# The layers' normalised input from the joined split parts of the turned x, in place of a second turn on TensorE

## The chip, the cores and the metric

One Trainium2 chip, one core (program of one core). The metric is device time in microseconds (us), the median of several executions. Engines: TensorE (PE, weight loads apart as PEld), VectorE (DVE), ScalarE (ACT), GpSimd (POOL) and the DMA queue of SyncE (SP).

## The reference, cut to what matters

A float32 network on 256 tokens of 2048 channels: a macaron block (feed-forward, token mixing, feed-forward), then two layers of a second block, each conditioned by an adaptive norm. The change touches only the opening of these two layers:

```python
for l in range(2):
    shift, scale, gate = split(silu(c) @ w_ada[l] + b_ada[l])          # per channel
    h = x * rsqrt(mean(x * x, axis=-1) + eps) * norm_g[l]              # per token rstd
    h = h * (1 + scale) + shift
    pieces = h @ w_in[l]                                               # 2048 x 6656, 13 pieces of 512
    ...                                                                # four mixers
    x = x + gate * (concat(mixers) @ w_out[l])
```

All products are done to float32 accuracy: both operands are split into a rounded high part and a low part, and three of the four partial products are summed.

## The kernel before, in words

The weights stream through as 1045 slabs of 512 KB. SP loads slab n into one of four stage buffers as soon as the low part of slab n - 4 is made. ScalarE rounds it into the high part (L1604), and GpSimd (L870, `rest`) or VectorE (L2111, `slab_lo`) subtracts to make the low part. TensorE runs the hi passes of a slab (16 products), waits for the low part, and runs the lo passes (8 products). Every engine works through an order of its own that is written out in the program; semaphores couple them.

A layer begins at slab `S_LAY[l]` (here called slab 0). Its h = x^T * gain * rstd + shift must lie with channels on partitions, and the sum over all channels that `rstd` needs is ready only when the last feed-forward or output group has been added to x. So the first two groups of products (8 slabs, `raw_product` with q = 0 and 1) run on the raw, unscaled turned x: `round_raw` (ScalarE) and `rest_raw` (VectorE, L2053) have made `hi + lo = x^T * gain`, block by block of 512 channels (`raw_views`). Blocks 0 to 2 are turned early; block 3 is turned by TensorE (`turn_raw`) behind slab 0. The results of the two groups are scaled by `rstd` afterwards (`raw_evacuate`).

The other groups take the real h. To make it, the kernel before computes `rstd` on VectorE from the sum of squares (`mean`, L1975, then `rstd_of`, L1981 to L1986: half, reciprocal, square, step, result; each two elements per partition), scales x by it per token (`scale_x`, L2071, 8 instructions of 128x512 a layer), turns the scaled x on TensorE once more (`turn_scaled`, transposes recorded at L908, 8 behind each slab of group 1), adds gain and shift on ScalarE (`gain_h`, L1664), and splits it on VectorE (`split_h`: casts L2063, subtract L2065). Group 2 waits for `h_ready` of each block.

`rstd` along the tokens of every partition (`rstd_b`) is made by two small diagonal matrices (`rdiag`, L2099), one product with ones behind group 0 (L1012) and a copy out of PSUM (L2517). The first two `turn_scaled` wait for that copy, since the banks of PSUM are shared.

In a layer VectorE makes the low parts of all input slabs but 0, 1, 6, 8 and 10, which are GpSimd's (`RAW_BY_POOL`). So between slab 1 and slab 6 GpSimd has nothing to do. On SP's queue the loads of the slabs and small rows of a bias table alternate; the other half of the rows is issued by GpSimd behind slab 10.

Of the kernel before, what the change touches and what calls it, by code (L numbers as in the profile page):

```python
# [283 lines left out]
def build(nc, a, out, const, marks, final):  # L284

    ctx = ExitStack()
    with ctx:
# [9 lines left out]
        def signal(name):  # L297
            return Signal(sem(name), marks.setdefault(name, {}), final)
# [77 lines left out]
        lgt, w2 = u(LGT, P, 3, 32), u(W2C, P, 2, 2, DH)  # L376
        y = u(CY, P, TT, D)
        yrs = u(YRS, P, S)
# [32 lines left out]
        def shifted(b):  # L411
            return u(LSQ + 1024 * (b % 2), P, 4, S)
# [19 lines left out]
        ada_split_done, ada_picked = sem("ada_split_done"), sem("ada_picked")  # L432
        block_turned = signal("block_turned")
        token_half, x_half, gained, h_rounded = (signal(n) for n in ("token_half", "x_half", "h_gained", "h_rounded"))
        h_ready, turned, squared, mean_done, root_done, rstd_ready, scaled, rounded = (signal(n) for n in (
# [430 lines left out]
        def _(pool):  # L866
            def rest(n):
# [3 lines left out]
                                        slab_part(n, 0, size(n)).bitcast(F32), ALU.subtract).then_inc(lo_pool, 1)  # L871

            for n in range(S_END):
                if n == S_MIX + 8:
                    pool.wait_ge(slab_done, S_MIX)
                    pool.wait_ge(ada_red, ADA_GROUPS)
                    pool.dma_start(U[:, DIST:DIST + MIX_END - BASE_END], const[:, BASE_END:MIX_END]).then_inc(mix_in, 16)
                    for kv in range(2):
                        pool.dma_start(w2[:, kv], a["cmp_w2"][0, kv].rearrange("(c p) n -> p c n", p=P)).then_inc(mix_in, 16)
# [7 lines left out]
                for l in range(2):  # L887
                    if n == S_LAY[l] + MASKED:
                        pool.wait_ge(*turned.after(3 + l, 3))
                        if l == 1:  # L890
# [12 lines left out]
        def _(pe):  # L903
# [77 lines left out]
            def raw_product(l, q):  # L981
# [5 lines left out]
                for k in range(4):  # L987
# [15 lines left out]
                    if q == 0 and k == 0:  # L1003
# [3 lines left out]
                        turn_raw(l, 3, 1).then_inc(*turned.mark("raw", l, 3))  # L1007
                    if q == 1:
                        turn_scaled(r, k)
                if q == 0:  # L1010
                    pe.wait_ge(*vec_out.after("rdiag", l))
                    mm(ps[:, 5, 0:S], ones, u(LNX, P, S), start=True, stop=True).then_inc(*pe_out.mark("scales", l))  # L1012

# [120 lines left out]
            def turn(r, b, src, T):  # L1134
# [3 lines left out]
                return last  # L1138

            def turn_scaled(r, b):  # L1140

                if b > 1:
                    pe.wait_ge(*gained.after(r, b - 2, 1))
                else:
                    pe.wait_ge(*vec_out.after("rstd_b", r - 3))
                for T in range(TT):
                    pe.wait_ge(*scaled.after(r, b, T))
                    last = turn(r, b, y, T)
                last.then_inc(*turned.mark(r, b))

# [432 lines left out]
        def _(act):  # L1583
# [72 lines left out]

            def gain_h(r, b, gain, shift):

                act.wait_ge(*turned.after(r, b))
                if b > 1:  # L1660
                    act.wait_ge(*h_ready.after(r, b - 2))
                for c in range(4):
                    m = 4 * b + c
                    last = fn(shifted(b)[:, c, :], turn_bank(r, b, c // 2)[:, c % 2, :], ACT.Identity, scale=gain[:, m:m + 1],  # L1664
                              bias=shift[:, m:m + 1])
                    if c % 2:
                        last.then_inc(*gained.mark(r, b, c // 2))
# [196 lines left out]
            for l in range(2):  # L1864
# [8 lines left out]
                for b in range(4):  # L1873
                    round_upto(s0 + 7 + b)
                    gain_h(3 + l, b, ascale[:, l, :], mod[:, l, 0:16])
                for p in range(PIECE + 1):
# [88 lines left out]
        def _(dve):  # L1965
# [101 lines left out]

            def scale_x(r, b):
                for T in range(TT):
                    cols = slice(b * WN, (b + 1) * WN)  # L2070
                    v.tensor_scalar(y[:, T, cols], x[:, T, cols], rstd[:, r, T:T + 1], None, ALU.mult).then_inc(*scaled.mark(r, b, T))  # L2071

# [16 lines left out]
            def norm_layer(l):  # L2089

                r, s0 = 3 + l, S_LAY[l]
                mean(r)
                rstd_of(r)
                dve.wait_ge(*rstd_ready.after(r))
                slab_lo(s0 + 2)
                rest_raw(l, 3)
                slab_lo(s0 + 3)
                for T in range(TT):
                    last = v.tensor_scalar(u(LNX, P, TT, P)[:, T, :], ident, rstd[:, r, T:T + 1], None, ALU.mult)  # L2099
                last.then_inc(*vec_out.mark("rdiag", l))  # L2100
                scale_x(r, 0)
                slab_lo(s0 + 4)
                for b in range(1, 4):
                    scale_x(r, b)
                slab_lo(s0 + 5)
# [398 lines left out]
            for l in range(2):  # L2504
# [6 lines left out]
                def raw_evacuate(q):  # L2511
# [3 lines left out]
                    if q == 0:  # L2515
                        dve.wait_ge(*pe_out.after("scales", l))
                        chained(v.tensor_copy(rstd_b[:, :], ps[:, 5, 0:S]), "rstd_b", l)  # L2517
                        dve.wait_ge(*vec_out.after("pad", l))
# [314 lines left out]
```

## Time and profile before

| | us |
|---|---|
| median of 3 runs | 3048.07 (3046.91 to 3048.76) |
| span of the profiled execution, first to last instruction | 3042.5 |
| median less span | 5.6 |
| TensorE busy in the span | 3022.6 (99%) |
| VectorE busy | 2007.6 (66%) |
| ScalarE busy | 1450.9 (48%) |
| GpSimd busy | 1305.0 (43%) |
| openings of layers 0 and 1 in the span | about 2171 to 2202 and 2600 to 2632 |

Times of the trace count from the start of the span. The span is one execution; the median is of others, so a forecast is made as a difference against the span and carried to the median.

### The profile page before, as it was taken

How to read it: one execution, taken by the hardware profiler on the slowest of the kernel's cores; microseconds unless marked ns; L12 is line 12 of the kernel's file. 1: busy time of each engine (PE TensorE's matmuls, PEld its weight loads, DVE VectorE, ACT ScalarE, POOL GpSimd, SP SyncE). 2: the span in 40 equal slices, each digit the busy share in tenths (PEclk: the TensorE clock that was granted, in tenths of full speed). 3: DMA queues.
4: the chain of work that ended last, by engine and by line, in shares of the span. 5: the costliest groups of instructions: out<-in, count | busy, mean ns of one | idle time of the engine just before them, and what ended most of it. 6: DMA issues, size and time to landing. Idle time of an engine off the chain costs nothing.

```text
span 3042.5 us, 46560 instructions
## 1 busy us (share of the span) xinstructions
PE 3022.6 (99%) x18776; PEld 2678.1 (88%) x18776; DVE 2007.6 (66%) x2956; ACT 1450.9 (48%) x1886; POOL 1305.0 (43%) x646
## 2 busy tenths in 40 slices
PE   9999999999999999999999999999999999999998
PEld 7888888888999999998888888888899998999997
DVE  4777666664324447786567666577579866689764
ACT  6444444444667455544544444444544454534454
POOL 5454545445565555594554444444350004510013
PEclk9999999999999999999999999999999999999999
DMA  7888887886776555555788888787576546665555
GB/s 233 277 277 259 270 281 250 286 288 180 229 174 177 157 167 147 155 171 194 231 269 275 271 268 269 259 287 267 172 213 193 156 144 214 175 191 181 153 179 181
DMA packets 495535, 663.28 MB, mean 218 GB/s; under 512 B 74312, under 2 KB 281912, under 8 KB 494808
## 3 DMA queue, kind: packets, MB, share of 16 engines
q1 hardware_dynamic: 485704, 655.83, 68.2%
q0 software_dynamic: 4448, 2.94, 0.3%
q8 instruction: 148, 2.42, 0.3%
q10 hardware_dynamic: 5168, 1.53, 0.2%
q14 instruction: 67, 0.55, 0.1%
HBM read 655.99 MB, written 2.11 MB: 216 GB/s over the span
## 4 chain that ended last, share of the span: by engine, by line
PE 97%; DMA 1%; DVE 1%; ACT 0%; POOL 0%; issue 0%; DVEq 0%; ACTq 0%
PE ps L1056 36%; PE ps L918 20%; PE ps L1061 18%; PE ps L924 10%; PE ps L935 3%; PE ps L940 1%; PE ps L908 1%; PE ps L1548 1%; DMA stage<-in_w_in 1%; PE ps L1332 1%; PE ps L1313 1%; PE ps L995 0%; PE ps L1027 0%; PE ps L1158 0%; POOL narrow_split_slabs L870 0%; PE ps L1370 0%
## 5 line engine op out<-in xcount | busy, mean ns | idle before, releaser
L870 POOL TENSOR_TENSOR split_slabs<-stage,split_slabs 128x1024 fp32r<-128x1024 f32 x318 | 777.6, 2446 | 1300.8 <-ACT split_slabs L1604 1300.6
L1604 ACT ACTIVATE split_slabs<-stage 128x1024 fp32r<-128x1024 f32 x592 | 627.4, 1061 | 870.4 <-PE ps L1061 813.5
L1056 PE MATMUL ps<-split_slabs,h_split 128*128 128x512 f32 x3288 | 813.6, 389 | 0.0
L1604 ACT ACTIVATE narrow_split_slabs<-stage 128x1024 fp32r<-128x1024 f32 (+1 forms) x437 | 457.3, 1051 | 620.4 <-PE ps L924 459.4
L1056 PEld LDWEIGHTS ps<-split_slabs,h_split 128*128 128x128 f32 x3288 | 616.8, 188 | 128.3
L2111 DVE TENSOR_TENSOR split_slabs<-stage,split_slabs 128x1024 fp32r<-128x1024 f32 x274 | 356.6, 1302 | 463.7 <-ACT split_slabs L1604 462.0
L918 PE MATMUL ps<-h_split,narrow_split_slabs 128*128 128x256 f32 x4928 | 623.6, 279 | 0.0
L918 PEld LDWEIGHTS ps<-h_split,narrow_split_slabs 128*128 128x128 f32 x4928 | 589.0, 188 | 11.5 <-issue 6.6
L870 POOL TENSOR_TENSOR narrow_split_slabs<-stage,narrow_split_slabs 128x1024 fp32r<-128x1024 f32 (+1 forms) x184 | 445.2, 2430 | 347.7 <-ACT narrow_split_slabs L1604 347.5
L1061 PE MATMUL ps<-split_slabs,h_split 128*128 128x512 f32 x1644 | 439.5, 389 | 0.0
L2111 DVE TENSOR_TENSOR narrow_split_slabs<-stage,narrow_split_slabs 128x1024 fp32r<-128x1024 f32 x253 | 329.2, 1304 | 138.2 <-ACT narrow_split_slabs L1604 137.8
L1061 PEld LDWEIGHTS ps<-split_slabs,h_split 128*128 128x128 f32 x1644 | 308.6, 188 | 64.4
L1056 PE MATMUL ps<-split_slabs,act_split 128*128 128x512 f32 x1392 | 344.1, 389 | 0.0
L924 PE MATMUL ps<-h_split,narrow_split_slabs 128*128 128x256 f32 x2464 | 332.7, 278 | 0.0
L1056 PEld LDWEIGHTS ps<-split_slabs,act_split 128*128 128x128 f32 x1392 | 261.3, 188 | 54.5
L924 PEld LDWEIGHTS ps<-h_split,narrow_split_slabs 128*128 128x128 f32 x2464 | 305.2, 188 | 0.0
L1061 PE MATMUL ps<-split_slabs,act_split 128*128 128x512 f32 x696 | 186.1, 389 | 0.0
L2173 DVE STREAM_TRANSPOSE ps<-U 32x256 f32<-32x256 f32 x352 | 160.3, 455 | 5.0
L1061 PEld LDWEIGHTS ps<-split_slabs,act_split 128*128 128x128 f32 x696 | 130.7, 188 | 27.3
L2127 DVE SCALAR_TENSOR_TENSOR ps<-U,cact,ps 128x512 f32<-128x512 f32 x192 | 145.1, 756 | 6.8
L2124 DVE SCALAR_TENSOR_TENSOR ps<-U,cact,ps 128x512 f32<-128x512 f32 x168 | 126.1, 751 | 22.5 <-DMA U<-in_w_ada 20.2
L2549 DVE SCALAR_TENSOR_TENSOR U<-U,params 128x256 f32<-128x256 f32 x240 | 112.1, 508 | 0.0
(307 smaller groups left out, 2540.2 us busy)
## 6 DMA issues: line engine op xcount, KB each, us to landing
stage<-in_ffn_w_gu SPq DMA_DIRECT2D x352, 512.0 KB, 4.9
stage<-in_w_in SPq DMA_DIRECT2D x349, 512.0 KB, 3.8
U<-in_w_ada SPq DMA_DIRECT2D x192, 512.0 KB, 5.4
stage<-in_ffn_w_down SPq DMA_DIRECT2D x176, 512.0 KB, 5.0
stage<-in_w_out SPq DMA_DIRECT2D x96, 512.0 KB, 4.1
stage<-in_w_in SPq DMA_DIRECT2D x80, 128.0 KB, 2.9
stage<-in_w_branch_c SPq DMA_DIRECT2D x32, 192.0 KB, 3.4
stage<-in_cmp_w SPq DMA_DIRECT2D x8, 512.0 KB, 5.1
```

Of the source, the lines that this page charges most:

```text
L870: nc.gpsimd.tensor_tensor(slab_part(n, 1, size(n)), stage[:, n % RING, 0:size(n)], slab_part(n, 0, size(n)).bitcast(F32), ALU.subtract).th ...
L918: mm(bank[:, c * S:(c + 1) * S], w[0][:, kk, at:at + P], moving(kk, i), start=first and c == 0 and kk == 0 and i == 0, stop=False)
L924: ins = mm(bank[:, c * S:(c + 1) * S], w[1][:, kk, at:at + P], moving(kk, 0), start=False, stop=last and c == outs - 1 and kk == chunks - 1)
L935: mm(bank[:, T * W2:(T + 1) * W2], hx[:, i, KC * k + kk, T * P:(T + 1) * P], w[0][:, kk, :], start=k + T + kk + i == 0, stop=False)
L1056: mm(ps[:, 2 * pair + T, :], stationary(kk, i)[:, T * P:(T + 1) * P], w[0][:, kk, :], start=first and kk == 0 and i == 0, stop=False)
L1061: ins = mm(ps[:, 2 * pair + T, :], stationary(kk, 0)[:, T * P:(T + 1) * P], w[1][:, kk, :], start=False, stop=last and kk == WK - 1)
L1604: return fn(slab_part(n, 0, size(n)), stage[:, n % RING, 0:size(n)], ACT.Copy)
L2111: v.tensor_tensor(slab_part(n, 1), stage[:, n % RING, :], slab_part(n, 0).bitcast(F32), ALU.subtract).then_inc(lo_vec, 1)
L2124: ins = v.scalar_tensor_tensor(total, w[:, 0, :], cact[:, 2 * k:2 * k + 1], total, ALU.mult, ALU.add)
L2127: v.scalar_tensor_tensor(total, w[:, 1, :], cact[:, 2 * k + 1:2 * k + 2], total, ALU.mult, ALU.add).then_inc(ada_load, 1)
L2173: last = v.transpose(dst[turned_rows, :, :, rows], src[rows, :, :, turned_rows])
L2549: ins = v.scalar_tensor_tensor(cy[:, c, :], src, col, cy[:, c, :], ALU.mult, ALU.add)
```

## The change

The second turn is dropped. Since the split parts of the raw turned x already add up to x^T * gain, GpSimd adds them back into one plain tensor (`join_raw`, 128x1024 a block, into `plain_h`, which takes the place of `y`); VectorE multiplies it in place by `rstd_b` (`scale_h`); ScalarE only adds the shift (`shift_h`). The split stays. In layer 0 the last 128 channels of the high part lie in a place of their own, so block 3 is joined in two pieces. GpSimd does the joins between its low parts of slabs 1 and 6. On TensorE the product that spreads the scales moves from behind slab 3 to behind slab 1, and on VectorE `rdiag` moves ahead of the low part of slab 2, the copy of `rstd_b` out of the evacuation of group 0 to behind the low part of slab 3. ScalarE does `shift_h` one slab earlier in its order than `gain_h` was.

```diff
+            def join_raw(l, b):
+                pool.wait_ge(*h_ready.after("raw", l, b))
+                m0, m1 = 4 * b, 4 * b + 4
+                if (l, b) == (0, 3):
+                    m1 = DC - 1
+                    nc.gpsimd.tensor_tensor(plain_h[:, m1, :], raw_part(l, 0, m1)[:, 0:S].bitcast(F32), raw_part(l, 1, m1)[:, 0:S].bitcast(F32), ALU.add
+                                            ).then_inc(*joined.mark(l, "last"))
+                lo_at = raw_views[l][2]
+                parts = [raw_views[l][0][:, at + m0 * XW:at + m1 * XW].rearrange("p (c w) -> p c w", c=m1 - m0)[:, :, 0:S].bitcast(F32) for at in (0, lo_at)]
+                nc.gpsimd.tensor_tensor(plain_h[:, m0:m1, :], parts[0], parts[1], ALU.add).then_inc(*joined.mark(l, b))
+
             for n in range(S_END):
+                for l in range(2):
+                    if n == S_LAY[l] + 2:
+                        pool.wait_ge(slab_done, S_LAY[l])
+                        for b in range(4):
+                            join_raw(l, b)
...
                     if n == S_LAY[l] + MASKED:
-                        pool.wait_ge(*turned.after(3 + l, 3))
+                        pool.wait_ge(*gained.after(3 + l, 3, 1))
...
-                    if q == 1:
-                        turn_scaled(r, k)
-                if q == 0:
-                    pe.wait_ge(*vec_out.after("rdiag", l))
-                    mm(ps[:, 5, 0:S], ones, u(LNX, P, S), start=True, stop=True).then_inc(*pe_out.mark("scales", l))
+                    if q == 0 and k == 1:
+                        pe.wait_ge(*vec_out.after("rdiag", l))
+                        mm(ps[:, 5, 0:S], ones, u(LNX, P, S), start=True, stop=True).then_inc(*pe_out.mark("scales", l))
...
-            def gain_h(r, b, gain, shift):
-                act.wait_ge(*turned.after(r, b))
+            def shift_h(r, b, shift):
+                act.wait_ge(*scaled.after(r, b))
...
-                    last = fn(shifted(b)[:, c, :], turn_bank(r, b, c // 2)[:, c % 2, :], ACT.Identity, scale=gain[:, m:m + 1],
-                              bias=shift[:, m:m + 1])
+                    last = fn(shifted(b)[:, c, :], plain_h[:, m, :], ACT.Identity, bias=shift[:, m:m + 1])
...
-                    round_upto(s0 + 7 + b)
-                    gain_h(3 + l, b, ascale[:, l, :], mod[:, l, 0:16])
+                    round_upto(s0 + 6 + b)
+                    shift_h(3 + l, b, mod[:, l, 0:16])
...
+            def scale_h(l, b):
+                dve.wait_ge(*joined.after(l, b))
+                if (l, b) == (0, 3):
+                    dve.wait_ge(*joined.after(l, "last"))
+                part = plain_h[:, 4 * b:4 * b + 4, :]
+                v.tensor_tensor(part, part, by_token(4), ALU.mult).then_inc(*scaled.mark(3 + l, b))
...
                 rstd_of(r)
                 dve.wait_ge(*rstd_ready.after(r))
+                for T in range(TT):
+                    last = v.tensor_scalar(u(LNX, P, TT, P)[:, T, :], ident, rstd[:, r, T:T + 1], None, ALU.mult)
+                last.then_inc(*vec_out.mark("rdiag", l))
                 slab_lo(s0 + 2)
                 rest_raw(l, 3)
                 slab_lo(s0 + 3)
-                for T in range(TT):
-                    last = v.tensor_scalar(u(LNX, P, TT, P)[:, T, :], ident, rstd[:, r, T:T + 1], None, ALU.mult)
-                last.then_inc(*vec_out.mark("rdiag", l))
-                scale_x(r, 0)
+                dve.wait_ge(*pe_out.after("scales", l))
+                chained(v.tensor_copy(rstd_b[:, :], ps[:, 5, 0:S]), "rstd_b", l)
+                for b in range(3):
+                    scale_h(l, b)
                 slab_lo(s0 + 4)
-                for b in range(1, 4):
-                    scale_x(r, b)
+                scale_h(l, 3)
                 slab_lo(s0 + 5)
```

## Rows read from the trace of the kernel before

**Rows 1.** The page: its head and the chain that ended last

```profile
span 3042.5 us, 46560 instructions
...
PE 97%; DMA 1%; DVE 1%; ACT 0%; POOL 0%; issue 0%; DVEq 0%; ACTq 0%
```

**Rows 2.** Waits of TensorE, 2165 to 3042: total, times, longest

```profile
PE ps L908 <- DVE rstd_b L2517: 4.0, 2, 2.3
```

**Rows 3.** Timeline of weight loads, layer 0: start, us, instructions, count, [idle before]

```profile
2178.40 1.98 PEld L995 LDWEIGHTS ps<-raw_split,narrow_split_slabs 128*128 128x128 f32 x16
...
2186.49 1.03 PEld L1000 LDWEIGHTS ps<-raw_split,narrow_split_slabs 128*128 128x128 f32 x8
2189.41 0.86 PEld L908 LDWEIGHTS ps<-base_consts,U 128*128 128x128 f32 x8 [1.90 <-DVE rstd_b L2517]
2190.23 1.98 PEld L995 LDWEIGHTS ps<-raw_split,narrow_split_slabs 128*128 128x128 f32 x16
...
2193.11 0.90 PEld L908 LDWEIGHTS ps<-base_consts,U 128*128 128x128 f32 x8
...
2193.98 1.97 PEld L995 LDWEIGHTS ps<-raw_split,narrow_split_slabs 128*128 128x128 f32 x16
```

**Rows 4.** The same timeline, layer 1

```profile
2606.79 2.00 PEld L995 LDWEIGHTS ps<-raw_split,narrow_split_slabs 128*128 128x128 f32 x16
...
2614.93 1.02 PEld L1000 LDWEIGHTS ps<-raw_split,narrow_split_slabs 128*128 128x128 f32 x8
2618.50 1.57 PEld L908 LDWEIGHTS ps<-base_consts,U 128*128 128x128 f32 x8 [2.55 <-DVE rstd_b L2517]
2620.05 2.72 PEld L995 LDWEIGHTS ps<-raw_split,narrow_split_slabs 128*128 128x128 f32 x16
```

**Rows 5.** Windows: busy us of each engine (count), granted clock, DMA share, GB/s

```profile
2187.52:2190.23 2.71, 1.02 (x9) 0.82 (x8) 2.68 (x9) 1.41 (x2) 2.28 (x1) 1.00 0.47 145
...
2615.95:2620.05 4.10, 1.76 (x10) 1.55 (x9) 3.18 (x9) 2.94 (x3) 1.65 (x1) 0.78 1.08 329
```

**Rows 6.** Timeline of VectorE in the openings of both layers

```profile
2173.76 0.17 DVE L1981 TENSOR_SCALAR newton<-meansq 128x2 f32<-128x2 f32 x1
...
2174.75 0.16 DVE L1986 SCALAR_TENSOR_TENSOR rstd<-newton 128x2 f32<-128x2 f32 x1
...
2178.39 1.23 DVE L2111 TENSOR_TENSOR narrow_split_slabs<-stage,narrow_split_slabs 128x1024 fp32r<-128x1024 f32 x1
...
2179.53 0.48 DVE L2099 TENSOR_SCALAR U<-base_consts,rstd 128x128 f32<-128x128 f32 x2
...
2189.00 0.36 DVE L2517 COPY rstd_b<-ps 128x256 f32<-128x256 f32 x1
...
2604.69 0.17 DVE L1981 TENSOR_SCALAR newton<-meansq 128x2 f32<-128x2 f32 x1
...
2607.18 1.66 DVE L2053 SCALAR_TENSOR_TENSOR raw_split<-ps,ascale,raw_split 128x256 fp32r<-128x256 f32 x4
```

**Rows 7.** Timeline of GpSimd in the openings of both layers

```profile
2170.56 2.41 POOL L870 TENSOR_TENSOR narrow_split_slabs<-stage,narrow_split_slabs 128x1024 fp32r<-128x1024 f32 x1 [0.31 <-ACT narrow_split_slabs L1604]
...
2187.95 3.22 POOL L870 TENSOR_TENSOR narrow_split_slabs<-stage,narrow_split_slabs 128x1024 fp32r<-128x1024 f32 x1 [14.98 <-ACT narrow_split_slabs L1604]
...
2601.69 2.39 POOL L870 TENSOR_TENSOR narrow_split_slabs<-stage,narrow_split_slabs 128x1024 fp32r<-128x1024 f32 x1 [1.76 <-ACT narrow_split_slabs L1604]
```

**Rows 8.** Timeline at two other places of the kernel, VectorE beside GpSimd

```profile
1198.01 2.36 DVE L2393 TENSOR_TENSOR rden<-rden,gn 128x6 f32<-128x6 f32 x1
...
1468.16 3.21 POOL L870 TENSOR_TENSOR split_slabs<-stage,split_slabs 128x1024 fp32r<-128x1024 f32 x1
1469.03 2.37 DVE L1981 TENSOR_SCALAR newton<-meansq 128x2 f32<-128x2 f32 x1
```

**Rows 9.** Timeline of ScalarE: the rounding of slab 6 in layers 0 and 1

```profile
2186.81 1.06 ACT L1604 ACTIVATE narrow_split_slabs<-stage 128x1024 fp32r<-128x1024 f32 x1 [1.14 <-DMA stage<-in_w_in]
...
2618.85 1.06 ACT L1604 ACTIVATE narrow_split_slabs<-stage 128x1024 fp32r<-128x1024 f32 x1 [0.53 <-DMA stage<-in_w_in]
```

More of the change, by code:

```diff
@@ L376, in build @@
         lgt, w2 = u(LGT, P, 3, 32), u(W2C, P, 2, 2, DH)
-        y = u(CY, P, TT, D)
+        plain_h = u(CY, P, DC, S)
         yrs = u(YRS, P, S)
@@ L433, in build @@
         block_turned = signal("block_turned")
+        joined = signal("raw_parts_joined")
         token_half, x_half, gained, h_rounded = (signal(n) for n in ("token_half", "x_half", "h_gained", "h_rounded"))
@@ L1138, in turn @@
                 return last
[L1140 to L1145, printed above, removed]
-                for T in range(TT):
-                    pe.wait_ge(*scaled.after(r, b, T))
-                    last = turn(r, b, y, T)
-                last.then_inc(*turned.mark(r, b))
             def ada_reduce(f, b):
@@ L2066, in split_h @@
                                 ).then_inc(*h_ready.mark(r, b))
[L2068 to L2071, printed above, removed]
+            def scale_h(l, b):
[4 more added lines that the diff above has]
+                v.tensor_tensor(part, part, by_token(4), ALU.mult).then_inc(*scaled.mark(3 + l, b))
             def norm_mix():
@@ L2097, in norm_layer @@
                 slab_lo(s0 + 3)
-                for T in range(TT):
-                    last = v.tensor_scalar(u(LNX, P, TT, P)[:, T, :], ident, rstd[:, r, T:T + 1], None, ALU.mult)
-                last.then_inc(*vec_out.mark("rdiag", l))
-                scale_x(r, 0)
+                dve.wait_ge(*pe_out.after("scales", l))
+                chained(v.tensor_copy(rstd_b[:, :], ps[:, 5, 0:S]), "rstd_b", l)
+                for b in range(3):
+                    scale_h(l, b)
                 slab_lo(s0 + 4)
-                for b in range(1, 4):
-                    scale_x(r, b)
+                scale_h(l, 3)
                 slab_lo(s0 + 5)
@@ L2515, in raw_evacuate @@
                     if q == 0:
-                        dve.wait_ge(*pe_out.after("scales", l))
-                        chained(v.tensor_copy(rstd_b[:, :], ps[:, 5, 0:S]), "rstd_b", l)
                         dve.wait_ge(*vec_out.after("pad", l))
```

## The prediction

> **What bounds the kernel now.** The chain that ended last is 97% TensorE, and the span is 3042.5 us [rows 1]. So only time in which TensorE waits or does other work than products can move the end. The view of waits, cut to the part from the last down-projection slab on, holds one line for TensorE: it waits for `rstd_b` (L2517), once in each layer, 4.0 us in all [rows 2]. Behind the layer openings it waits for nothing, so a shift of TensorE there goes through to the end at full size. I then read the two openings in the timeline by engine.
>
> In layer 0 slab 4 (the first of raw group 1) is done at 2186.49 + 1.03 = 2187.52, the first `turn_scaled` starts at 2189.41 after 1.90 us idle, and slab 5 starts at 2190.23 [rows 3]. A raw slab takes 2193.11 - 2190.23 = 2.88 us (24 weight loads, the last 8 need the slab's low part), a turned block of 8 transposes 2193.98 - 2193.11 = 0.87 us. Layer 1 is alike, but its wait is 2.55 us, and there the first block takes 1.57 us instead of 0.87 and the next 16 weight loads 2.72 us instead of 1.98 [rows 3, 4]. The view of windows tells why: the granted clock of that stretch is 0.78 of full speed (half speed, 1.2 GHz, for part of it), and 1.00 in layer 0's [rows 5]. So this dip costs 0.70 + 0.74 = 1.4 us.
>
> **What the change removes.** 64 transposes and both waits. Layer 0: 1.90 + 0.82 + 3 x 0.87 = 5.3 us. Layer 1: 2.55 + 1.4 + 4 x 0.87 = 7.4 us. In all 12.7 us, if nothing else comes late. The scales product only moves, and 16 `scale_x` of 0.48 us on VectorE turn into 8 `scale_h` of the size of a slab's low part, 1.23 us [rows 6]: 2 us more on VectorE. ScalarE's `shift_h` reads SBUF in place of PSUM, taken as equal; it now stands one slab earlier in the queue and has its input long before. SP's order of issues is the same, but its load of slab 6 waits for slab 2's low part, of slab 7 for slab 3's, of slab 8 for slab 4's; POOL's bias rows wait for the last `shift_h` in place of the last turn, and nothing near is queued behind them.
>
> **What it adds.** GpSimd gets four joins per layer (layer 0: the last in two pieces). The nearest row is its own low-part subtract, the same two inputs in SBUF and 128x1024: 2.41 us [rows 7]; I take that, with 0.6 and 1.8 us for the pieces. Before, GpSimd was idle 14.98 us there, from 2172.97 on [rows 7]. The joins of blocks 0 to 2 wait for data ready long ago, so they run back to back behind slab 1's low part: 2173.0 to 2180.2, and in layer 1 2604.1 to 2611.3.
>
> That is when VectorE works out `rstd`: L1981 starts at 2173.76 and 2604.69 and L1986 gives `rstd` 1 us later [rows 6]. These instructions have two elements a partition and no wait between the engines is written. But what the trace shows of such an overlap is decisive [rows 8]: at 1469.03 the same L1981 took 2.37 us, until the GpSimd subtract that began at 1468.16 was done (1471.37); at 1198.01 a 6-element tensor_tensor took 2.36 us beside another. The other way round, the GpSimd subtract at 2187.95 took 3.22 us beside VectorE's low part. The copy out of PSUM at 2189.00, in the middle of that subtract, took its 0.36 us [rows 6, 7]. I read: a VectorE instruction with two SBUF inputs, or a tensor_scalar from SBUF to SBUF, and a GpSimd subtract exclude each other for their whole length; one with a PSUM operand is free. A waiting engine comes next when the other finishes, so back-to-back joins let one such VectorE instruction through each.
>
> The Trainium skill, "SBUF — State Buffer", section "Who interferes with whom", speaks against the change in the same sense: the shared pair of ports is held for a whole instruction, by GpSimd or by a VectorE instruction that has two SBUF inputs or a two-port mode. If only the two-port modes excluded GpSimd, and two SBUF inputs did not, the sum would be that of the third rival below; the row at 1198.01 is against that.
>
> **Layer 0, step by step.** L1981 waits out join 0 (2175.4), the square L1984 join 1 (2177.85), the step L1985 join 2 (2180.3); `rstd` 2180.5 in place of 2174.9; the two halves of `rdiag` 0.48 us [rows 6], 2181.0. TensorE now wants `rdiag` behind slab 1, at 2178.40 [rows 3]: it waits 2.6 us, does the scales product (0.3) and slab 2 and 3, until 2187.05. VectorE goes on: low part of slab 2, 2182.2; `rest_raw` 4 products, 1.66 us [rows 6], 2183.9 (slab 3 needs it at 2184.2); low part of slab 3, 2185.15; copy, 2185.5. Now three `scale_h` and the low part of slab 4, 4 x 1.2 us, and between them what GpSimd has: the small piece of join 3 (0.2 more), the large one (1.8), and the subtract of slab 6. Slab 6's rounding started on its DMA at 2186.81 [rows 9]; its load now leaves at 2182.3, so I put the rounded slab at 2188.5, when `scale_h` 1 has the turn, and the subtract (2.4) goes ahead of `scale_h` 2. Sum: 2185.5 + 4.8 + 0.2 + 1.8 + 2.4 = 2194.7, about 2194.6. TensorE wants this low part at 2187.05 + 1.95 = 2189.0: it idles 5.6 us. Then 0.96 for the rest of slab 4 and 3 x 2.88 for slabs 5 to 7: group 2 starts at 2204.2, against 2193.98 + 2 x 2.88 + 2 x 0.87 = 2201.5 before: +2.7. Idle of 2.55 us was followed by the half clock, of 1.90 us not [rows 3 to 5]; 5.6 us therefore costs 1.4 more: **+4.1**.
>
> **Layer 1.** `rstd` 2611.6 and `rdiag` 2612.1; TensorE wants it at 2606.8 [rows 4] and idles 5.3 us; with a dip of 1.4 it has slab 3 done at 2619.6 and wants slab 4's low part at 2621.6. VectorE: slab 2's low part 2613.3, `rest_raw` 2615.0, slab 3's low part 2616.2; join 3 is whole (2.4), `scale_h` 0 at 2619.7, `scale_h` 1 at 2620.9; slab 6 is rounded at 2618.85 + 1.06 = 2619.9 [rows 9], its subtract goes next, 2623.3; `scale_h` 2 and the low part: 2625.7. Plus 0.96 + 8.64 + 1.4 is 2636.7, against 2620.05 + 0.74 + 3 x 2.88 + 3 x 0.87 = 2632.0 before: **+4.7**. The later steps (splits of h, slab 11's low part) come out within a microsecond of their need by the same durations; taken as nothing, bounds 0 and +2 a layer. Were the waits of `rstd` all, TensorE's first idle would give back 2.6 + 5.3 us of the 12.7 and the second nothing; it is the second that turns the sign.
>
> Sum +8.8 us: the profiled execution's 3042.5 becomes 3051.3; the median of the runs stands 5.6 us above that span, so 3048.07 + 8.8 = **3056.9 us**. Its own range: without the clock dips of the second idle -2.8, without slab 6's subtract ahead in one layer -2.4 (3051.7); late splits +4 (3061).
>
> **Rivals.** 0.2% (6.1 us) is about what a measurement of this kernel can tell from no change.
> 1. *The joins disturb nothing that matters* (they start later, or let short VectorE instructions in). Then slab 4's low part comes at about 2185.4 where TensorE wants it at 2186.5: all 12.7 us are won, 3035.4. It decides at `rstd`: it holds if that is ready by about 2176, so at most one join may stand before it. For it: 14.98 us of idle GpSimd. Against: rows 8. Chance 0.17, faster.
> 2. *The waits come, but mildly*: slab 6's subtract comes after slab 4's low part in both layers (2 x 2.4 less) and no dip in clock is paid (2.8 less). 8.8 - 7.6 = +1.2, 3049. Chance 0.14, the same.
> 3. *Only tensor_scalar is shut out.* `rstd` at 2176.2, but `rdiag`'s two halves wait out joins 1 and 2: 2180.4. Then `scale_h` runs freely, slab 4's low part is there at 2189.7 and 2620.8: layer 0 1.4 us of second idle, -2.2, layer 1 -1.7: 3044.2. Chance 0.06, the same.
> 4. *A train of late parts*: the splits of h and slab 11's low part also come late, 3 us or more a layer: 3063. Chance 0.06, slower.
> The forecast has 0.57. Faster 0.17, same 0.20, slower 0.63. The range of 3042 to 3063 takes in the mild cases and leaves out most of rival 1 and the tail of rival 4.
>
> **What the profile after would show.** L1981, L1984 and L1985 at 1.7 to 2.4 us each in the layers; L1986 near 2180.5 and 2611.6; TensorE idle for `rdiag` behind slab 1 (2.6 and 5.3 us) and for slab 4's low part (5.6 and 4.1 us); a half clock behind them in both layers; GpSimd's joins at 2.4 us, some longer beside VectorE. Wrong it would be if the newton rows stay at 0.16 us, if the joins start after them, or if slab 6 is rounded only after slab 4's low part.

## The result and the profile after

The changed kernel took 3051.22 us (median of 12 runs, 3048.59 to 3054.54), the kernel before 3048.82 us on the same chip (12 runs, 3045.42 to 3052.16). The ratio is 1.0016, 95% interval 1.0008 to 1.0023: slower, by 0.16%, which is inside the 0.2% taken as the bound of "the same". In a second comparison on another chip (the last experiment below) it was 1.0008, 0.9999 to 1.0016. The forecast was +8.8 us. The medians say +2.4 and +2.8, the two ratios +4.9 and +2.4, and the two profiles (spans 3042.5 and 3046.8) +4.3. The profiled execution of the changed kernel took 3048.59 us. The head of its page:

```profile
span 3046.8 us, 46426 instructions
PE 3017.2 (99%) x18712; PEld 2672.8 (88%) x18712; DVE 2023.0 (66%) x2948; ACT 1448.3 (48%) x1886; POOL 1326.8 (44%) x655
```

TensorE is busy 5.4 us less than before (3022.6) in a span that is 4.3 us longer: 9.7 us more of idle.

The waits of TensorE from 2165 us to the end, changed kernel (total us, times, longest):

```profile
PE ps L1028 <- DVE U L2103: 6.9, 2, 4.8
PE ps L1018 <- DVE narrow_split_slabs L2120: 5.6, 2, 4.3
PE ps L936 <- DVE h_split L2069: 0.8, 1, 0.8
PE ps L942 <- DVE narrow_split_slabs L2120: 0.5, 1, 0.5
```

The one line of before [rows 2], 4.0 us in two waits, has become four lines, 13.8 us in six. L1028 is the scales product, which waits for `rdiag` (L2103); L1018 are the lo passes of the raw slabs. So the change removed 64 transposes and two waits and paid 13.8 us of new waits.

VectorE in the opening of layer 0 (timeline: start, us, engine, line):

```profile
2173.88 1.61 DVE L1985 TENSOR_SCALAR newton<-meansq 128x2 f32<-128x2 f32 x1
2175.52 0.17 DVE L1987 RECIPROCAL newton<-root 128x2 f32<-128x2 f32 x1
2175.72 2.10 DVE L1988 TENSOR_TENSOR newton<-newton 128x2 f32<-128x2 f32 x1
2177.86 2.29 DVE L1989 TENSOR_TENSOR newton<-newton 128x2 f32<-128x2 f32 x1
2180.19 0.16 DVE L1990 SCALAR_TENSOR_TENSOR rstd<-newton 128x2 f32<-128x2 f32 x1
2180.38 0.48 DVE L2103 TENSOR_SCALAR U<-base_consts,rstd 128x128 f32<-128x128 f32 x2
...
2185.07 7.32 DVE L2078 TENSOR_TENSOR U<-U,rstd_b 128x1024 f32<-128x1024 f32 x3
2192.32 1.21 DVE L2120 TENSOR_TENSOR narrow_split_slabs<-stage,narrow_split_slabs 128x1024 fp32r<-128x1024 f32 x1
```

GpSimd beside it:

```profile
2173.04 7.09 POOL L884 TENSOR_TENSOR U<-raw_split 128x1024 f32<-128x1024 f32 x3
2183.65 1.55 POOL L880 TENSOR_TENSOR U<-raw_split_last,raw_split 128x256 f32<-128x256 f32 x1 [3.51 <-DVE raw_split L2057]
2185.16 2.86 POOL L884 TENSOR_TENSOR U<-raw_split 128x768 f32<-128x768 f32 x1
2188.58 2.73 POOL L871 TENSOR_TENSOR narrow_split_slabs<-stage,narrow_split_slabs 128x1024 fp32r<-128x1024 f32 x1 [0.56 <-ACT narrow_split_slabs L1609]
```

Three instructions of two elements, 0.16 us each before [rows 6], now take 1.61, 2.10 and 2.29 us: each stands until one of the three joins of 7.09 / 3 = 2.36 us is done. `rstd` comes at 2180.35. Then three `scale_h` take 7.32 us instead of 3 x 1.2, since join 3 and slab 6's subtract (2188.58) stand between them.

TensorE's weight loads, layer 0:

```profile
2180.92 0.30 PEld L1028 LDWEIGHTS ps<-U,base_consts 128*128 128x128 f32 x2 [2.33 <-DVE U L2103]
2181.24 2.08 PEld L1013 LDWEIGHTS ps<-raw_split,narrow_split_slabs 128*128 128x128 f32 x16
...
2193.58 1.61 PEld L1018 LDWEIGHTS ps<-raw_split,narrow_split_slabs 128*128 128x128 f32 x8 [4.52 <-DVE narrow_split_slabs L2120]
2195.07 2.96 PEld L1013 LDWEIGHTS ps<-raw_split,narrow_split_slabs 128*128 128x128 f32 x16
```

The same view, layer 1:

```profile
2615.06 0.50 PEld L1028 LDWEIGHTS ps<-U,base_consts 128*128 128x128 f32 x2 [4.99 <-DVE U L2103]
2615.65 3.78 PEld L1013 LDWEIGHTS ps<-raw_split,narrow_split_slabs 128*128 128x128 f32 x16
2619.30 1.57 PEld L1018 LDWEIGHTS ps<-raw_split,narrow_split_slabs 128*128 128x128 f32 x8
...
2630.11 1.01 PEld L1018 LDWEIGHTS ps<-raw_split,narrow_split_slabs 128*128 128x128 f32 x8 [1.52 <-DVE narrow_split_slabs L2120]
...
2647.32 1.91 PEld L936 LDWEIGHTS ps<-h_split,narrow_split_slabs 128*128 128x128 f32 x16 [0.96 <-DVE h_split L2069]
...
2650.83 1.32 PEld L936 LDWEIGHTS ps<-h_split,narrow_split_slabs 128*128 128x128 f32 x11
```

Idle of 2.33 us left the next 16 loads at 2.08 us; idle of 4.52 and of 4.99 us was followed by loads at up to twice their time. The windows say that this is the clock (columns as in [rows 5]; 0.79 and 0.61 are means of full and half speed):

```profile
2192.00:2200.00 8.00, 6.42 (x41) 6.42 (x42) 7.82 (x16) 3.36 (x6) 0.00 (x0) 0.79 0.55 158
...
2615.00:2622.00 7.00, 6.94 (x35) 6.76 (x36) 6.97 (x9) 0.81 (x1) 3.29 (x1) 0.61 0.71 193
```

The length of the idle does not settle whether the clock falls. A second profile of the changed kernel (the last experiment below), weight loads:

```profile
2181.39 0.30 PEld L1028 LDWEIGHTS ps<-U,base_consts 128*128 128x128 f32 x2 [2.34 <-DVE U L2103]
2181.72 2.92 PEld L1013 LDWEIGHTS ps<-raw_split,narrow_split_slabs 128*128 128x128 f32 x16
...
2194.07 1.01 PEld L1018 LDWEIGHTS ps<-raw_split,narrow_split_slabs 128*128 128x128 f32 x8 [3.02 <-DVE narrow_split_slabs L2120]
...
2632.09 1.02 PEld L1018 LDWEIGHTS ps<-raw_split,narrow_split_slabs 128*128 128x128 f32 x8 [3.03 <-DVE narrow_split_slabs L2120]
```

There an idle of 2.34 us was followed by the half clock (granted clock 0.70 from 2180.50 to 2186.20), one of 3.02 us was not (1.00 from 2192 to 2200), and one of 3.03 us was again (0.72 from 2632 to 2638).

A measure free of what happened earlier in the run is the time from a layer's first raw weight load (L995, L1013 after: 2171.78 and 2603.28) to the first of group 2 and of group 3 (2650.83 in the last row of layer 1 above). From the timelines:

| us | layer 0: group 2 | group 3 | layer 1: group 2 | group 3 |
|---|---|---|---|---|
| before | 29.81 | 40.71 | 31.99 | 43.30 |
| after | 32.86 | 43.80 | 33.91 | 47.55 |
| difference | +3.1 | +3.1 | +1.9 | +4.3 |
| after, second profile | 31.41 | 44.73 | 35.70 | 47.01 |
| difference | +1.6 | +4.0 | +3.7 | +3.7 |

At group 3 the two openings together cost 7.4 us in one execution and 7.7 in the other; how this divides between the layers and the steps differs.

### The profile page after: what moved, and what is told of

It reads as the page before. It is cut to its first block and busy times, and to the rows that moved or that the text cites. A ratio compares the mean times of both kernels' runs of the same rounds, so it can differ in the third digit from the quotient of the medians.

```text
span 3046.8 us, 46426 instructions
## 1 busy us (share of the span) xinstructions
PE 3017.2 (99%) x18712; PEld 2672.8 (88%) x18712; DVE 2023.0 (66%) x2948; ACT 1448.3 (48%) x1886; POOL 1326.8 (44%) x655
## 5 line engine op out<-in xcount | busy, mean ns | idle before, releaser
L936 PE MATMUL ps<-h_split,narrow_split_slabs 128*128 128x256 f32 x4928 | 622.5, 279 | 0.9 <-DVE h_split L2069 0.8
L936 PEld LDWEIGHTS ps<-h_split,narrow_split_slabs 128*128 128x128 f32 x4928 | 587.9, 188 | 12.9 <-issue 6.8
L942 PE MATMUL ps<-h_split,narrow_split_slabs 128*128 128x256 f32 x2464 | 332.3, 277 | 0.6 <-DVE narrow_split_slabs L2120 0.5
L942 PEld LDWEIGHTS ps<-h_split,narrow_split_slabs 128*128 128x128 f32 x2464 | 304.5, 188 | 1.0 <-DVE narrow_split_slabs L2120 0.7
```

The lines of the kernel that those rows point to most:

```text
L936: mm(bank[:, c * S:(c + 1) * S], w[0][:, kk, at:at + P], moving(kk, i), start=first and c == 0 and kk == 0 and i == 0, stop=False)
L942: ins = mm(bank[:, c * S:(c + 1) * S], w[1][:, kk, at:at + P], moving(kk, 0), start=False, stop=last and c == outs - 1 and kk == chunks - 1)
```

## The experiments

"Before" is the kernel before, run on the same chip beside the variants (medians 3049.75, 3048.9, 3045.63 and 3049.49 us in the four comparisons). A gain or loss in us is the ratio's, if nothing else is said. "Openings" are the times to group 2 and group 3 as in the table above, in the one profiled execution.

### The adds alone, in the kernel before

```diff
+  if n == S_LAY[l] + 2:            # GpSimd, in the kernel before
+      pool.wait_ge(slab_done, S_LAY[l])
+      for b in range(3): tensor_tensor(unused rows, hi part, lo part, ADD)
```

> The kernel before, with three of the new GpSimd adds per layer (blocks 0 to 2, same inputs, same place in GpSimd's order; results are written to free memory and not used). Theory (GpSimd's adds and VectorE's instructions with two SBUF inputs exclude each other): the first newton row and the two tensor_tensor rows behind it take 1.6 to 2.3 us each, rstd is ready 5.4 us later than before (near 2180.2 and 2611.3), slab 2's low part is late for TensorE by 1.2 and 4.0 us, the first second turn starts 1.8 us later in layer 0 and 2.7 us net in layer 1: +4.5 us. Rival (the adds are harmless, the changed kernel loses its time through the new order of VectorE and TensorE): newton rows 0.16 us, 0 us.

Measured: 3055.53 us, ratio 1.0018 (1.0009 to 1.0027), +5.5 us by the ratio. VectorE's timeline in it, layer 0:

```profile
2177.48 1.61 DVE L1992 TENSOR_SCALAR newton<-meansq 128x2 f32<-128x2 f32 x1
...
2179.32 2.10 DVE L1995 TENSOR_TENSOR newton<-newton 128x2 f32<-128x2 f32 x1
2181.45 2.33 DVE L1996 TENSOR_TENSOR newton<-newton 128x2 f32<-128x2 f32 x1
```

Nobody uses these sums, and neither VectorE nor TensorE is made to wait for them (ScalarE's first `gain_h` waits for the third, which is done long before its turn comes). The same three rows are as long as in the changed kernel: the exclusion is shown. The openings to group 2 are 4.9 and 1.7 us longer than before, where 1.8 and 2.7 were expected; layer 0 also ran at half clock behind its 3.58 us of idle for `rstd_b`.

### The change without any join

```diff
-  pool: join_raw(l, b)                                       # all four
-  v.tensor_tensor(part, part, by_token(4), MULT)
+  v.tensor_tensor(part, high part of raw x, by_token, MULT)  # low part left out
```

> The changed kernel without the GpSimd adds: VectorE's scaling reads the high parts of the raw x directly (this leaves the low parts out of h, so the result is a little less exact); everything else as changed. Theory (exclusion by the adds): nothing is late, rstd near 2174.9, slab 4's low part at 2185.4 where TensorE wants it at 2186.5, all waits in the openings gone: -12.7 us against before. Rival (VectorE's chain of work in the new order is too long by itself): TensorE still waits some microseconds for slab 4's low part in both layers, between -6 and 0 us.

Measured: 3038.88 us, ratio 0.9968 (0.9956 to 0.9979), -9.8 us. So it is the joins that turn the sign. But the gain is not the 12.7 us of the removed turn: the openings to group 3 are 1.7 and 3.3 us shorter than before, 5.0 in all, since waits are left (2.7 us for high parts, 1.7 + 1.5 + 0.4 for low parts and splits, 6.3 in all). The next run keeps the second turn and gains nearly as much.

### The scales moved, the second turn kept

```diff
   for k in range(4):
+      if q == 0 and k == 1: wait rdiag; scales product     # was behind slab 3
...
   rdiag; slab_lo(2); rest_raw; slab_lo(3)                  # rdiag was behind them
+  copy of rstd_b                                           # was in the evacuation of group 0
```

> The kernel before with the second half of the change alone: rdiag ahead of slab 2's low part, the scales product behind slab 1, the copy of rstd_b behind slab 3's low part; second turns stay, no GpSimd adds. Theory: the wait for rstd_b goes in both layers (1.90 and 2.55 us) and with it layer 1's dip in clock (1.4 us): -5.9 us. Rival (another wait, for the scaled x or a bank of PSUM, takes its place): 0 to -2 us.

Measured: 3041.6 us, ratio 0.9973 (0.9963 to 0.9983), -8.2 us. TensorE's waits, as above:

```profile
PE ps L995 <- ACT narrow_split_slabs L1604: 1.7, 2, 1.0
PE ps L940 <- DVE narrow_split_slabs L2113: 0.4, 1, 0.4
PE ps L918 <- DVE h_split L2065: 0.2, 1, 0.2
```

The 4.0 us for `rstd_b` are gone, and layer 1's half clock with them. The openings to group 3 are 1.0 and 2.3 us shorter than before: the expected 5.9 us, less new idle of 2.5 us. This is one part of the change, a few moved lines, and it beats both kernels. Against it the run without joins, which drops all 64 transposes, is only 1.6 us better by the ratios (with overlapping intervals; not at all against the repeat below, 0.9968) and 1.7 by the openings: the dropped turn itself was worth little here, even before the joins are paid.

### The joins on VectorE

```diff
-  pool: join_raw(l, b)
+  dve: tensor_tensor(plain_h[b], hi, lo, ADD)   # right ahead of each scale_h
```

> The changed kernel with the joins done by VectorE (1.22 us each, ahead of each scaling) in place of GpSimd. Theory (what costs is GpSimd's 2.4 us adds shutting VectorE out, not the adding): rstd on time; VectorE's own chain gives slab 4's low part at 2188.5, 2.1 us late for TensorE, slab 5's 0.7 us late, then in time; group 2 starts 2.7 us earlier than before in each layer: -5.5 us against before, about 10 us faster than the changed kernel. Rival (VectorE's load is what costs): 8 more instructions on VectorE make it slower than the changed kernel.

Measured: 3049.53 us, ratio 1.0000 (0.9992 to 1.0009). That is not clear of the changed kernel's 1.0016 and 1.0008, and not below the kernel before by the 5.5 us expected. The waits for low parts stay (L1013, 8.0 us, 4 times, longest 3.9): an add takes 1.22 us on VectorE and 2.36 on GpSimd, but either way it lies in the time before slab 4's low part.

### The joins held back until `rdiag` is made

```diff
   pool.wait_ge(slab_done, S_LAY[l])
+  pool.wait_ge(*vec_out.after("rdiag", l))
```

> The changed kernel, GpSimd's joins held back until rdiag is made, so that none can stand before the newton rows. Theory (the exclusion costs wherever a join meets a VectorE instruction with two SBUF inputs, and it is the sum up to slab 4's low part that counts): newton rows back at 0.16 us, no wait for rdiag behind slab 1, but the four joins now stand between slab 2's low part and slab 4's; that comes near 2192.2 in layer 0, TensorE waits some 5.8 us there, group 2 starts about 2 us later than before in each layer: +3 to +4 us against before, 1 to 4 us better than the changed kernel. Rival (only the delay of rstd costs; the rest fits beside the products): -10 us against before, like the kernel without joins.

Measured: 3052.74 us, ratio 1.0011 (1.0002 to 1.0020). TensorE's waits and a row of GpSimd's timeline:

```profile
PE ps L1019 <- DVE narrow_split_slabs L2121: 11.8, 2, 9.0
```

```profile
2176.45 9.95 POOL L884 TENSOR_TENSOR U<-raw_split 128x1024 f32<-128x1024 f32 x3 [2.59 <-PE ps L1019]
```

The three small VectorE rows are back at 0.16 to 0.17 us, no wait for `rdiag` is left, and the 11.8 us for low parts stand against 6.9 + 5.6 = 12.5 in the changed kernel. So a late `rstd` is not the only cost: without it the joins' own time costs as much, since they still stand ahead of slab 4's low part.

### The gate's copy later: with the scales moved, and without joins

With the scales moved, the rounding of slab 4 waits for its load, behind ScalarE's copy of the layer's gate to memory (8 KB in scattered elements). ScalarE's timeline in that run:

```profile
2173.08 0.39 ACTq L1868 DMA_DIRECT2D gate_row<-mod  x1
...
2187.94 1.06 ACT L1604 ACTIVATE narrow_split_slabs<-stage 128x1024 fp32r<-128x1024 f32 x1 [5.95 <-DMA stage<-in_w_in]
```

The copy was moved to piece 5 of the layer:

```diff
-  act.dma_start(gate_row[l], mod[:, l, 32:48])    # at the layer's start
...
+      if p == 5: act.dma_start(gate_row[l], mod[:, l, 32:48])
```

> The kernel of the moved scales (second turns kept, no joins), and ScalarE issues the small scattered transfer of the gate row behind group 4 instead of at the layer's start. Theory (in the opening slabs 4 to 6 now wait for their DMA, which the gate row's thousands of tiny packets hold up for 12 us): slab 4 is rounded before TensorE has finished slab 3, the remaining waits for high parts (1.7 us by the profile) go: 2 us better than the moved scales alone, -10 us against before. Rival (the weight stream itself is what is late): the same as the moved scales alone.

> The changed kernel without the adds (VectorE scales the high parts, the low parts are left out of h), gate row later: the most that dropping the second turns could give. Theory: -13 us against before (12.7 of the forecast's sum, less late splits, plus what the DMA held up). Rival: as the run without joins, -10 us.

Measured: 3045.12 us, ratio 0.9990 (0.9981 to 0.9999), and 3044.16 us, 0.9983 (0.9974 to 0.9992): in the first comparison the copy at its old place gave 0.9973 and 0.9968, both better, with intervals that just overlap. The openings did get shorter (38.85 and 39.24 us to group 3 where the scales are moved, from 39.75 and 40.97), but a wait came where the copy now stands: for high parts, 4.4 us, longest 3.0, and 3.8 us in the run without joins. The expectation was wrong: a hold-up of the slab stream was moved, not removed.

### ScalarE takes block 3, VectorE joins the others

```diff
+  act: for c in range(4): plain_h[12 + c] = ascale * PSUM block      # block 3, no join
+  dve: join and scale blocks 0 and 1; slab_lo(4); slab_lo(5); blocks 2 and 3
-  pool: join_raw(l, b)
```

> No second turns and no work of GpSimd for them: ScalarE writes block 3 of the plain gained x from PSUM, VectorE joins blocks 0 to 2, the low parts of slabs 4 and 5 stand ahead of the scaling of blocks 2 and 3, the gate row later. Theory: the waits for slab 4's low part (8.0 us in the run with VectorE's joins) go, what stays late is the split of h, some 2 us a layer: -8 us against before, so about equal to the moved scales. Rival (VectorE's load in the opening is too high in any order): near 0, as with VectorE's joins.

> The variant in which ScalarE scales block 3 out of PSUM and VectorE joins and scales blocks 0 to 2, with the gate's copy back at its old place at the layer's start, so that it differs from the changed kernel in the joins alone. Theory: the later copy cost 3.5 us in the pair of runs that differ in it alone with the scales moved, and 4.6 in the pair without joins; taken back, 2.7 above the kernel before becomes 1 to 2 below it. Rival: the copy at its old place holds slabs 4 and 5 back as it did in the others, their low parts come later again, and nothing is won: 2 to 3 above.

Measured: 3051.48 us with the later copy, ratio 1.0009 (1.0001 to 1.0018), and 3046.12 us, 1.0001 (0.9992 to 1.0010), with the copy back at its place. The first expectation (-8) was wrong; the second run came out at neither end (its median +0.5, between -1 to -2 and +2 to +3), and the intervals overlap. Its waits are 5.7 us for raw low parts (3 times, longest 2.3) and 3.4 in small ones. No ordering tried pays for the joins.

### Layer 0's copy in the mixing stage

```diff
-  at layer 0's start: act.dma_start(gate_row[0], mod[:, 0, 32:48])
+  behind the last unit of the mixing stage: the same
```

> The kernel before with the scales moved ahead of slab 2's low part (as in the run with the scales moved alone), and layer 0's copy of its gate to memory, 8 KB in scattered elements, issued by ScalarE at the end of the mixing stage, where the DMA engines are busy a smaller share; layer 1's copy stays where it was. Theory: in layer 0 the roundings of slabs 4 to 6 no longer wait for their loads, which shortened that opening by 0.9 us when the copy was issued later (27.94 against 28.84 us to group 2), and no stall comes back later in the layer: about 9 us below the kernel before, 1 below the run with the scales moved alone. Rival: the copy holds up the loads just as much where it now stands, and TensorE waits there some 3 us: about 5 us below the kernel before.

Measured: 3047.06 us, ratio 1.0001 (0.9992 to 1.0010). ScalarE's timeline around the copy's new place:

```profile
1302.89 0.39 ACTq L1851 DMA_DIRECT2D gate_row<-mod  x1
...
1317.96 1.06 ACT L1604 ACTIVATE narrow_split_slabs<-stage 128x1024 fp32r<-128x1024 f32 x1 [7.94 <-DMA stage<-in_w_branch_b]
```

The opening of layer 0 is as short as expected (27.94 us to group 2, 38.85 to group 3), and the rival's mechanism is there as well: a rounding waits 7.94 us for its load, TensorE's weight loads stand still for 2.96 us, and the next 16 take 3.14 us instead of 1.89. That is more than 4 us. But neither size came (-9, or -5 by the rival): the 8 us lost against the runs with the scales moved are not all found, and the profiled execution (3044.41 us) is no slower than theirs (3045.46 and 3044.26).

### The scales moved, and the changed kernel, once more side by side

> The run with the scales moved alone, word for word, once more and beside the changed kernel. The run with layer 0's gate copied earlier came out 0.4 us above the kernel before, on a chip where the kernel before took 3045.6 instead of 3049.75 us; its trace shows a wait of 2.8 us behind the copy, which accounts for part only. Theory: the gain of 8 us belongs to the kernel and comes again, 6 to 10 us below the kernel before. Rival: it hangs on the chip and on the pace at which TensorE happens to run, and is 4 us or less here.

> The changed kernel itself, beside the run above. Theory: 2 to 7 us above the kernel before, as in its first comparison (ratio 1.0016), so 8 to 15 us above the run with the scales moved alone. Rival: on the chip it is as fast as the kernel before, and the first ratio was that chip's.

Measured: 3040.82 us, ratio 0.9968 (0.9956 to 0.9981), and 3052.28 us, ratio 1.0008 (0.9999 to 1.0016); by the medians -8.7 and +2.8 us. Both theories held: the gain comes again, and the two kernels stand 11.5 us apart. Two profiles of the same changed code have spans of 3046.8 and 3054.1 us with the same sums of waits (L1028 6.9, L1018 5.6, L936 0.8, L942 0.5). Of the 7.3 us between them, 6.4 arise behind group 3's start in the two layers (2.9 and 3.5), and there it is TensorE's pace. Weight loads in layer 1, first execution:

```profile
2660.80 0.98 PEld L942 LDWEIGHTS ps<-h_split,narrow_split_slabs 128*128 128x128 f32 x8
...
2663.52 0.98 PEld L942 LDWEIGHTS ps<-h_split,narrow_split_slabs 128*128 128x128 f32 x8
```

The second execution:

```profile
2673.40 1.01 PEld L942 LDWEIGHTS ps<-h_split,narrow_split_slabs 128*128 128x128 f32 x8
...
2676.23 1.01 PEld L942 LDWEIGHTS ps<-h_split,narrow_split_slabs 128*128 128x128 f32 x8
```

A slab takes 2663.52 - 2660.80 = 2.72 us in one and 2676.23 - 2673.40 = 2.83 us in the other, with no idle in either. Both run at full clock; a window of 50 us, first in the first execution:

```profile
2655.00:2705.00 50.00, 50.00 (x444) 50.00 (x442) 35.10 (x46) 20.67 (x20) 22.00 (x45) 1.00 0.77 219
```

and in the second:

```profile
2655.00:2705.00 50.00, 50.00 (x427) 50.00 (x426) 32.02 (x42) 21.39 (x21) 25.28 (x52) 1.00 0.76 218
```

TensorE is never idle and the granted clock is 1.00 in both, but it does 444 products in one and 427 in the other.

## Why the prediction was right, and where it was not

**What bounds the kernel, and what the change removes.** TensorE's waits decide, and the 12.7 us are rightly added up, but their condition ("if nothing else comes late") is not met even without joins: the run without them gains 9.8 us, of which the openings show 5.0, and some 8 to 10 come with the moved scales alone.

**The exclusion.** Right to 0.4 us. The measured times are the first profile's; in layer 1 those of `rstd`, `rdiag` and slab 4's low part are less 3.21 us, by which that layer's first raw load came later (2603.28 against 2600.07).

| | forecast, layers 0 / 1 | measured |
|---|---|---|
| `rstd` ready | 2180.5 / 2611.6 | 2180.35 / 2611.3 |
| `rdiag` ready | 2181.0 / 2612.1 | 2180.9 / 2611.8 |
| idle for `rdiag` | 2.6 / 5.3 | 2.33 / 4.99 |
| slab 4's low part ready | 2194.6 / 2625.7 | 2193.5 / 2622.4 |
| idle for it | 5.6 / 4.1 | 4.52 / 0; slab 5's 1.52 |
| loss by half clock | 1.4 / 1.4 and 1.4 | 1.5 / 2.5 and 0 |
| start of group 2 | +4.1 / +4.7 | +3.1 / +1.9 |

The clock's loss is worked out from the loads: layer 0, 1.61 + 2.96 against 1.03 + 1.99; layer 1, 0.50 + 3.78 + 1.57 against 0.30 + 2.00 + 1.03. The forecast took from one idle of 2.55 us (half clock) and one of 1.90 us (none) that every longer one brings it; the second profile's 2.34 us (half clock) and 3.02 us (none) are against that, so these sizes fit in part by luck. The section that the prediction cites (the Trainium skill, "SBUF — State Buffer", "Who interferes with whom") and these rows agree, 2.10 and 2.29 us for two elements; the rival by which only tensor_scalar is shut out falls, since the tensor_tensor rows L1988 and L1989 are the longest.

**Layer 0.** The term that was too large is the stretch of three `scale_h`, the rest of join 3 and slab 6's subtract: 3 x 1.2 + 0.2 + 1.8 + 2.4 = 8.0 us forecast, 7.32 measured, and the copy before it ended 0.4 us earlier. The subtract went ahead of `scale_h` 2, as forecast.

**Layer 1.** The step that was wrong is "slab 6 is rounded at 2618.85 + 1.06 = 2619.9 [rows 9], its subtract goes next". It holds two mistakes. The row at 2618.85 [rows 9] is slab 7's rounding; slab 6's is the one ahead of it, kernel before:

```profile
2617.26 1.06 ACT L1604 ACTIVATE narrow_split_slabs<-stage 128x1024 fp32r<-128x1024 f32 x1 [0.49 <-DMA stage<-in_w_in]
```

And after the change neither time is the DMA's any more. ScalarE's timeline, changed kernel:

```profile
2621.19 1.06 ACT L1609 ACTIVATE narrow_split_slabs<-stage 128x1024 fp32r<-128x1024 f32 x1 [8.71 <-PE ps L1018]
2624.08 1.06 ACT L1609 ACTIVATE narrow_split_slabs<-stage 128x1024 fp32r<-128x1024 f32 x1 [1.83 <-PE ps L1018]
```

Slabs 5 and 6 wait for TensorE to finish slabs 2 and 3, whose split places they take: TensorE's own delay of 5 us pushes the rounding back. So slab 6 is ready only at 2625.1. VectorE's making of slab 4's low part and GpSimd's subtract of slab 6:

```profile
2624.36 1.21 DVE L2120 TENSOR_TENSOR narrow_split_slabs<-stage,narrow_split_slabs 128x1024 fp32r<-128x1024 f32 x1
...
2625.22 2.61 POOL L871 TENSOR_TENSOR narrow_split_slabs<-stage,narrow_split_slabs 128x1024 fp32r<-128x1024 f32 x1 [4.14 <-ACT narrow_split_slabs L1609]
```

The subtract comes behind slab 4's low part, not ahead, and makes slab 5's low part late by 1.52 us instead of slab 4's by 4.1. The prediction's second rival has this order in both layers. But the order is not the kernel's own. In the second profile, layer 1:

```profile
2628.58 2.38 POOL L871 TENSOR_TENSOR narrow_split_slabs<-stage,narrow_split_slabs 128x1024 fp32r<-128x1024 f32 x1 [3.19 <-ACT narrow_split_slabs L1609]
...
2628.66 3.37 DVE L2120 TENSOR_TENSOR narrow_split_slabs<-stage,narrow_split_slabs 128x1024 fp32r<-128x1024 f32 x1
```

Here the subtract is ahead by 0.08 us and slab 4's low part takes 3.37 us instead of 1.21: TensorE waits 3.03 us, and the half clock comes a second time, as forecast. Group 2 starts 3.7 us later than before in that execution, 1.9 in the other. A forecast of one order for such a near race could hit or miss by chance.

**"The later steps taken as nothing, bounds 0 and +2 a layer".** Mis-sized in one layer: in the first profile the splits of h and two low parts came late by 0.21 + 0.30 + 0.96 + 0.68 us in layer 1, from +1.9 at group 2 to +4.3 at group 3, and in layer 0 it is 0. In the second profile it is layer 0 that goes from +1.6 to +4.0. So the two layers cost 3.1 + 4.3 = 7.4 us at group 3 (7.7 in the second), against the 8.8 forecast, with errors of both signs in it.

**From 7.4 us to the spans' 4.3.** Nothing in the sum foresaw this. In layer 0 the two kernels take the same time from group 3 to layer 1's first raw load, 387.70 us. In layer 1 the changed kernel (in its first profile) takes 3.2 us less from group 3 to the end: the kernel before runs at 2.83 us a slab up to about 2722, the changed one at 2.72, which is some 28 slabs x 0.11 = 3.1 us. Since the second profile of the changed kernel has the slow pace in both layers, this belongs to the execution as far as the runs show, and not to the change.

**What stays open.** The medians give +2.4 and +2.8 us where the openings give 7.4 and 7.7; unprofiled runs have no trace, and how often each has which pace isn't known. By the openings the forecast of +8.8 is near; by the medians its second rival (+1.2) is nearer. The same holds for the runs with the scales moved: their openings to group 3 are 3.3 and 3.6 us shorter than before's in sum, out of 8 to 10 us, and where the rest comes from is not shown. Their profiled executions were the slowest of their runs both times (3045.46 of a median of 3041.6, 3044.26 of 3040.82), and reached layer 0 3.6 and 3.0 us later than the kernel before's, with a stretch of half clock about 855 us (granted clock 0.83 from 850 to 860 us, 1.00 in the kernel before), where the code is the same. The kernel before had its profile in an execution under its median (median less span 5.6 us, against 4.4 in the changed kernel's first comparison and -1.8 in its second).

## What to carry to other kernels

An idle engine is not free capacity where it shares a path with the one that sets the pace: count the two engines' time on that path as one sum. Here holding the joins back removed one wait (6.9 us) and lengthened the other by nearly as much (5.6 to 11.8 us). Try the parts of a change apart: the small part, the scales moved ahead, gave 8 to 10 us in two comparisons, and the large one adds at most some 1.6 us without its joins and gives all of it away with them. And when a forecast carries times over from a trace, ask of each of them what would release it after the change, since a row that waited for a DMA may wait for the delayed engine itself. Where two instructions come within a fraction of a microsecond of each other on a shared path, give the price of both orders.

## What was not expected of the hardware

**Two paces at the full clock.** With the granted clock at 1.00 and no idle, three groups (12 slabs) behind a layer's opening took 32.64 us or 33.92 us (2.72 or 2.83 us a slab). The pace of a stretch differs between executions of the same code. What sets it is open.

**A small transfer that holds up large ones.** The gate's copy of 8 KB (2064 packets) was followed by a rounding that waited 7.94 us for its load, in a stretch where the DMA engines were busy 0.60 of the time (1303 to 1318 us), and in the layers by a rounding that waited 5.95 us; with the copy moved away, slab 4's rounding in layer 0 waited for no load. Each of the three places it was given had its cost.
